# Attention: a third of the modulation in the context tile's units, and the copies of the two heads' probabilities exchanged between ScalarE and VectorE

## The reference

```python
shift1, scale1, gate1, shift2, scale2, gate2 = jnp.split(silu(c) @ w_ada[l] + b_ada[l], 6)   # for c and for c_ctx
h = rms_norm(x, norm1) * (1 + scale1) + shift1
q, k, v, su, sv, cb, cc, cx = jnp.split(h @ w_in, offs, axis=-1)      # 1024 x 2048
q, k = rms_norm per head; latent tokens get rotary positions
s = einsum(q, k_all) * scale; p = softmax(s); attn = einsum(p, v_all) # 8 heads of 64, 2 key heads
merged = [rms_norm(attn), rms_norm(chunk_sgu(su, sv)), rms_norm(conv(cb, cc, cx))]
x = x + gate1 * (merged @ w_out)                                      # 1024 x 1024
h2 = rms_norm(x, norm2) * (1 + scale2) + shift2
x = x + gate2 * hierarchical_moe(h2)                                  # 16 experts, 2 per token
```

## Time and profile before

| | us |
|---|---|
| Median of three runs | 1143.53 (1143.19 to 1144.98) |
| Profiled execution, its own time | 1145.23 |
| Its span in the profile | 1143.4 |
| TensorE busy | 945.5 (83%) |
| VectorE busy | 668.8 (58%) |
| ScalarE busy | 589.6 (52%) |
| GpSimd busy | 264.2 (23%) |
| Mean granted clock of TensorE | 0.908 of the full one |
| Attention, first to last maximum, layer 0 | 168.92 to 271.06 |
| Attention, first to last maximum, layer 1 | 717.91 to 820.27 |

### The profile page before, as it was taken

One profiled execution on the slowest core, in us unless ns is written; L12 is line 12 of the kernel. 1 busy time (PEld: TensorE's weight loads), 2 busy tenths in 40 slices (PEclk: granted clock), 3 DMA queues, 4 the chain that ended last, 5 costly groups with the idle time before them and its releaser, 6 DMA issues.

```text
span 1143.4 us, 14987 instructions
## 1 busy us (share of the span) xinstructions
PE 945.5 (83%) x5232; PEld 742.3 (65%) x5232; DVE 668.8 (58%) x929; ACT 589.6 (52%) x900; POOL 264.2 (23%) x306
## 2 busy tenths in 40 slices
PE   3799989996998599999139999899789849999910
PEld 0488865764886378887128887576578738888710
DVE  0349225654374599998354841455536579998736
ACT  1662235655321388887266322565533328988722
POOL 3024016212140122220330500721204122222033
PEclk9999997999998599999659999799989869999965
DMA  9955213473235999999661321266324539999653
GB/s 323 273 206 211 74 51 148 167 296 113 88 141 181 368 339 410 418 413 321 205 230 61 109 89 29 81 255 245 125 92 148 183 106 380 400 418 410 269 188 124
DMA packets 85951, 248.36 MB, mean 217 GB/s; under 512 B 25644, under 2 KB 30252, under 8 KB 75656
## 3 DMA queue, kind: packets, MB, share of 16 engines
q1 hardware_dynamic: 72760, 209.54, 48.6%
q0 software_dynamic: 11696, 32.86, 8.4%
q10 hardware_dynamic: 1440, 5.24, 1.1%
HBM read 221.07 MB, written 30.21 MB: 220 GB/s over the span
## 4 chain that ended last, share of the span: by engine, by line
PE 72%; DVE 10%; DMA 7%; ACT 5%; issue 4%; POOL 1%; SPq 0%; DVEq 0%; ACTq 0%; POOLq 0%
PE ps L1375 12%; PE ps L1377 12%; PE ps L1376 12%; PE ps L1382 4%; PE ps L1384 4%; PE ps L1383 4%; PE ps L1525 4%; PE ps L1392 4%; PE ps L1510 3%; DMA pool<-in_moe_w 3%; DMA raw<-in_w_ada 2%; PE ps L1499 2%; PE ps L1640 2%; PE ps L1500 2%; DVE wL L1232 1%
## 5 line engine op out<-in xcount | busy, mean ns | idle before, releaser
L1375 PE MATMUL ps<-wH,actH 128*128 128x512 f32 x608 | 248.8, 409 | 13.6 <-DVE actL L1321 12.2
L1377 PE MATMUL ps<-wH,actL 128*128 128x512 f32 x608 | 242.2, 398 | 0.0
L1376 PE MATMUL ps<-wL,actH 128*128 128x512 f32 x608 | 241.3, 397 | 0.0
L1232 DVE TENSOR_TENSOR wL<-raw,wH 128x2048 fp32r<-128x2048 f32 x64 | 146.1, 2283 | 11.4 <-ACT wH L858 11.2
L1375 PEld LDWEIGHTS ps<-wH,actH 128*128 128x128 f32 x608 | 117.4, 193 | 38.3 <-issue 13.3
L858 ACT ACTIVATE wH<-raw 128x2048 fp32r<-128x2048 f32 x64 | 122.2, 1910 | 27.6 <-DMA raw<-in_moe_w 27.6
L1377 PEld LDWEIGHTS ps<-wH,actL 128*128 128x128 f32 x608 | 116.8, 192 | 26.1
L1376 PEld LDWEIGHTS ps<-wL,actH 128*128 128x128 f32 x608 | 117.4, 193 | 22.8
L1382 PE MATMUL ps<-wH,actH 128*128 128x512 f32 x256 | 105.3, 411 | 8.2 <-DVE actL L1310 5.3
L1112 DVE TENSOR_REDUCE nmax<-ps 128x1 f32<-128x640 f32 (+1 forms) x80 | 57.1, 714 | 80.7 <-PE ps L1500 80.5
L1384 PE MATMUL ps<-wH,actL 128*128 128x512 f32 x256 | 102.2, 399 | 0.0
(11 more groups left out here) (226 smaller groups left out, 1576.8 us busy)
## 6 DMA issues: line engine op xcount, KB each, us to landing
raw<-in_w_ada SPq DMA_DIRECT2D x48, 1024.0 KB, 7.9
raw<-in_moe_w SPq DMA_DIRECT2D x96, 512.0 KB, 7.6
raw<-in_w_in SPq DMA_DIRECT2D x16, 1024.0 KB, 9.0
raw<-in_moe_w SPq DMA_DIRECT2D x16, 1024.0 KB
pool<-in_moe_w SPq DMA_DIRECT2D x32, 512.0 KB
pool<-in_moe_w SPq DMA_DIRECT2D x16, 1024.0 KB, 11.5
ys<-pool SPq DMA_DIRECT2D x32, 512.0 KB, 10.4
raw<-in_w_out SPq DMA_DIRECT2D x8, 1024.0 KB, 8.2
```

Of the source, the lines that this page charges most:

```text
L1232: dve.tensor_tensor(wL[:, i, :], mraw[parity][i], f32(wH[:, i, :]), ALU.subtract).then_inc(sem(f"m_lo{i}"), 1)
L1375: pe.matmul(out, aH, wH[:, slot_, cols_], start=first, stop=False)
L1376: pe.matmul(out, aH, wL[:, slot_, cols_], start=False, stop=False)
L1377: return pe.matmul(out, aL, wH[:, slot_, cols_], start=False, stop=last)
```

## The change

- `ADA_AT`: the sixteen modulation units of attention were a third list in tile 1 (two each in units 10 and 11, one each in 12 to 15) and in tile 3 (units 26 to 31). After the change eight are in the context tile (one each in units 2 to 5, two each in 6 and 7) and eight in tile 2 (units 18 to 23). The pieces are complete in units 7 and 23 instead of 15 and 31.
- Piece 1 and its bias move to a region that holds the `sgu_w` weights until they are transposed, and the bias is added in place. Its load on GpSimd moves from after the convolution to before it. `piece_out` of piece 1 and the bias load of piece 2 move before the first statistics; the latter waits for the convolution instead of piece 1.
- The copy of the transposed probabilities of odd heads goes from VectorE to ScalarE, behind the copy of the output, and that of even heads from ScalarE to VectorE, behind the maximum.
- Weight unit w 8 is split in unit 33 instead of 36, and w 9 in unit 37 instead of the merge's chunk 1.

```diff
--- before.py
+++ after.py
@@ -184,8 +184,9 @@
         frow = tabs[:, :, :, :, :].rearrange("p t a b d -> p (t a b d)")[:, 0:D]
-        piece = [misc[:, 0:N], aux[:, 2560:3072], aux[:, 2560:3072]]
-        bpiece = [misc[:, N:2 * N], aux[:, 3072:3584], aux[:, 3072:3584]]
+
+        piece = [misc[:, 0:N], misc[:, 768:1280], aux[:, 2560:3072]]
+        bpiece = [misc[:, N:2 * N], misc[:, 768:1280], aux[:, 3072:3584]]
         mraw = [[raw[:, 0, :], raw[:, 1, :], raw[:, 2, :]],
@@ -236,9 +237,9 @@
         none, third = (0,) * NH, (0, 0, 2, 2, 1, 1, 1, 1)
-        ADA_AT = none + third + none + third + none
+        ADA_AT = (0, 0, 1, 1, 1, 1, 2, 2) + none + third + none + none
         PIECE_AT = [u for u in range(NT * NH) if ADA_AT[u] and sum(ADA_AT[:u + 1]) % KD == 0]
-        W_AT = {36: 8}
+        W_AT = {33: 8, 37: 9}
         def ada_bank(l, q):
@@ -469,9 +470,9 @@
             def bias_in(l, q):
                 if q == 1:
+                    pl.wait_ge(sem("sgT_psum"), at("sgT_psum", l, 1))
+                elif q == 2:
                     pl.wait_ge(sem("conv_done"), at("conv_done", l, 1))
-                elif q == 2:
-                    pl.wait_ge(sem("piece_done"), at("piece_done", l, q))
                 for j in range(4):
                     c = q * U + j * N
                     pl.dma_start(bpiece[q][32 * j:32 * j + 32, :], I["b_ada"][l, c:c + N].partition_broadcast(32)).then_inc(sem("bias_in"), 16)
@@ -501,6 +502,7 @@
                     c = 8 * (i % 2)
                     rstd(stat[:, 16 + c:16 + c + n], stat[:, 32 + c:32 + c + n], n, HD, sem("ssqk"), at("ssqk", l, i + 1), sem("rqk"))
+                bias_in(l, 1)
                 tap = lambda w: cw[:, w, :].unsqueeze(1).to_broadcast([P, NT, 256])
                 pl.wait_ge(sem("shifted"), at("shifted", l, 96))
                 pl.wait_ge(sem("taps_loaded"), at("taps_loaded", l, 32))
@@ -525,11 +527,10 @@
                     link(pl.tensor_scalar(stat[:, c:c + 2], stat[:, c:c + 2], 1.0 / 256, EPS, ALU.mult, ALU.add))
                     pl.tensor_tensor(stat[:, c + 16:c + 18], stat[:, c:c + 2], nhalf[:, 0:2], ALU.pow).then_inc(sem("rstd3b"), 1)
-                bias_in(l, 1)
+                piece_out(l, 1)
+                bias_in(l, 2)
                 rest_stats(0)
                 attn_stats(0)
-                piece_out(l, 1)
-                bias_in(l, 2)
                 rest_stats(1)
                 attn_stats(1)
                 rest_stats(2)
@@ -765,16 +766,16 @@
                 q_out(0, 1)
                 q_hi(1)
                 for u in range(NT * NH + 4):
-                    if u % 2 == 0 and 2 <= u < NT * NH + 2:
+                    if u % 2 and u >= 5:
+                        oT_out((u - 5) // 2)
+                    if u % 2 and 3 <= u < NT * NH + 2:
                         w = u - 2
                         keys = 5 * P if w >= NH else P
                         act.wait_ge(sem("pT_psum"), at("pT_psum", l, w + 1))
                         if w >= 4:
                             act.wait_ge(sem("pv"), at("pv", l, w // 2 - 1))
-                        act.activation(pT[w // 2 % 2][:, 0, 0:keys], flat[:, 4 * N:4 * N + keys], ACT.Copy).then_inc(sem("pT"), 1)
-                    elif u % 2 and u >= 5:
-                        oT_out((u - 5) // 2)
+                        act.activation(pT[w // 2 % 2][:, 1, 0:keys], flat[:, 4 * N:4 * N + keys], ACT.Copy).then_inc(sem("pT"), 1)
                     if u < NT * NH:
                         t, h = divmod(u, NH)
                         keys = 5 * P if t else P
@@ -807,8 +808,6 @@
                     on = cols[:, k:k + 1]
                     act.activation(actHk[:, k, 0:512], ps[:, 5 + 2 * (k % 2), :], ACT.Identity, scale=on).then_inc(sem("mT_hi"), 1)
                     act.activation(actHk[:, k, 512:640], ps[:, 6, 0:P], ACT.Identity, scale=on).then_inc(sem("mT_hi"), 1)
-                    if k == 1:
-                        split_hi(9)
                 for i in range(10, 12):
                     split_hi(i)
@@ -953,9 +952,7 @@
                 dve.wait_ge(sem("ada_read"), at("ada_read", l, KD * (q + 1)))
                 dve.wait_ge(sem("bias_in"), at("bias_in", l, 64 * (q + 1)))
-                if q == 2:
-                    dve.wait_ge(sem("piece_out"), at("piece_out", l, 64))
-                elif l:
+                if l:
                     dve.wait_ge(sem("piece_out"), at("piece_out", l, 0))
                 dve.tensor_tensor(piece[q], ps[:, ada_bank(l, q), :], bpiece[q], ALU.add).then_inc(sem("piece_done"), 1)
@@ -1110,14 +1107,14 @@
                         if u >= 2:
                             dve.wait_ge(sem("prob"), at("prob", l, u - 1))
                         dve.tensor_reduce(nmax[:, u % 2:u % 2 + 1], flat[:, 2 * N * (u % 2):2 * N * (u % 2) + keys], X, ALU.max, negate=True).then_inc(sem("nmax"), 1)
-                    if u % 2 and 3 <= u < NT * NH + 2:
+                    if u % 2 == 0 and 2 <= u < NT * NH + 2:
                         w = u - 2
                         keys = 5 * P if w >= NH else P
                         dve.wait_ge(sem("pT_psum"), at("pT_psum", l, w + 1))
                         if w >= 4:
                             dve.wait_ge(sem("pv"), at("pv", l, w // 2 - 1))
-                        dve.tensor_copy(pT[w // 2 % 2][:, 1, 0:keys], flat[:, 4 * N:4 * N + keys]).then_inc(sem("pT"), 1)
+                        dve.tensor_copy(pT[w // 2 % 2][:, 0, 0:keys], flat[:, 4 * N:4 * N + keys]).then_inc(sem("pT"), 1)
                     if u % 2 and u >= 5:
                         pair_out((u - 5) // 2)
                     if u in W_AT:
@@ -1142,8 +1139,6 @@
                     dve.scalar_tensor_tensor(out=actLk[:, k, 512:640], in0=ps[:, 6, 0:P], scalar=on,
                                              in1=f32(actHk[:, k, 512:640]), op0=ALU.mult, op1=ALU.subtract
                                              ).then_inc(sem("mT_lo"), 1)
-                    if k == 1:
-                        split_lo(9)
                 for i in range(10, 12):
                     split_lo(i)
```

## The result

The changed kernel takes 1153.51 us in the median of five runs, against 1144.77 for the kernel before in its five: 1.0086 of the time, 95% interval 1.0068 to 1.0103, so 9 to 10 us slower (8.7 by the medians, 9.8 by the ratio). The profiled execution has a span of 1151.1 us, 7.7 more than before. My range ended at 1151.5 and my forecast was no change.

What follows compares the result with a forecast made beforehand. TensorE, with 72% of the chain, was taken to bound the kernel. Modulation -2.25, splits +3.5 and tail -0.55 gave +0.7 us a layer, +1.4 in all: 1144.9 us, no change that could be told, range 1138 to 1151.5.

Steps and rivals of the forecast that it cites:

- The context tile: Eight modulation units enter it; first latent maximum at 189.6 instead of 181.61, 8.0 us lost a layer (bounds 4.5 to 12).
- the splits' term for the clock: Tile 4: 1.2 falls of the clock for 1 now, 0.3 us a layer.
- Tile 1: Becomes plain when its modulation leaves: 15.2 us instead of 23.85, 8.65 gained a layer.
- Copies exchanged: Pairs without modulation: 4.56 to 4.29 us, 0.27 off each; queries' low part 0.5 off in tiles 1 and 2 without modulation.
- Modulation moved: Context and latent tiles: 8.0 us lost, 8.65 and 1.6 gained, so 2.25 gained a layer.
- rival 2: Clock stays low through the context tile: 6.0 us a layer slower, 1157 us; chance 0.08.
- the 10 that I had named as a sign of being wrong: Prediction called wrong if the context tile grows by under 5 or over 10 us.
- Rival 3: Context tile's last load at 188.2 and a clock fall for each stall: 1.8 us a layer slower, 1148.5; chance 0.14.
- Splits: Tile 4: TensorE stands 3.5 us in one piece; 3.5 lost a layer, and nothing gained in the merge.
- Rival 1: Second split, in unit 37, is cheap: 1140.7 us at half price, 1136.5 at none; chance 0.26.
- Tail: Last copy goes to ScalarE while VectorE divides the pair before: 0.55 us gained a layer (0 to 0.8).
- Bias load, GpSimd's and SyncE's queues: Earlier bias load covered by GpSimd's wait for shifted rows, SyncE's loads not late, later GpSimd issues cost nothing.

Runs made afterwards that it cites:

- e6_ex_mod: Kernel before with the copies exchanged and the modulation moved, splits as before (unit 36 and merge): 1136.5 us, 0.9931 of the kernel before.
- e7_short_loads: Kernel before with copies exchanged and modulation moved, loads of modulation units 12 to 15 cut to one eighth of their bytes: 1128.1 us, 0.9855.
- e4_w9_back: The changed kernel with w 9 split in the merge again, w 8 still in unit 33: 1144.5 us, 1.0001 of the kernel before.
- e1_exchange: Kernel before with only ScalarE's and VectorE's copies exchanged: 1131.1 us, 0.9890 of the kernel before.
- e5_ex_33: Kernel before with the copies exchanged and w 8 split in unit 33 instead of 36: 1139.4 us, 0.9961 of the kernel before.
- e11_ex_34: Kernel before with the copies exchanged and w 8 split in unit 34 instead of 36: 1132.7 us, 0.9892 of the kernel before.
- e2_modulation: Kernel before with only the modulation moved, with piece 1's new places and GpSimd's new order: 1152.6 us, 1.0073 of the kernel before.
- e10_even: The changed kernel with its two splits one unit later, in units 34 and 38: 1149.1 us, 1.0051 of the kernel before.

## Why the prediction was wrong

Step by step, with the sum of +0.7 a layer against +5.4 and +5.1. Two steps failed. The context tile came out 2.2 and 1.5 over its term, because the clock fell again in the waits for the last loads. And the splits' term for the clock, "1.2 falls of the clock for 1", was too small: the clock fell behind both splits, and the second fall shows in the tail, 1.7 and 2.0 over its term. Tile 1 adds 0.7 and 0.5.

*Copies exchanged.* Right. A plain pair took 4.27 where I had 4.29 (4.56 before). The transposes of two even units, with ScalarE's copy of the odd unit between, in the changed kernel's list of instructions (start, us of it, engine and line, operation, out <- in; in brackets what it waited for and how long):

```profile
237.56 0.73 PE L1505 MATMUL ps<-ident,pool 128*128 128x128 f32 x5
...
240.20 0.74 PE L1505 MATMUL ps<-ident,pool 128*128 128x128 f32 x5
...
240.98 0.71 ACT L778 ACTIVATE pool<-ps 128x640 f32<-128x640 f32 x1 [1.12 <-PE ps L1505]
...
241.83 0.73 PE L1505 MATMUL ps<-ident,pool 128*128 128x128 f32 x5
```

*Modulation moved.* This step failed in the size of two terms, the context tile and what follows it. TensorE's part went as forecast and better: unit 8 of the modulation at 172.12 took 1.94, and the clock was back by 174.6 already, so rival 2 did not happen. The early clock was partly luck, as the last section shows. But then it waited for each of the last loads:

```profile
172.12 1.94 PE L1387 MATMUL ps<-raw,cpad 128*32 128x512 f32 x8
...
174.64 1.06 PE L1387 MATMUL ps<-raw,cpad 128*32 128x512 f32 x8
...
182.39 1.07 PE L1387 MATMUL ps<-raw,cpad 128*32 128x512 f32 x8 [1.35 <-DMA raw<-in_w_ada]
...
184.91 1.94 PE L1387 MATMUL ps<-raw,cpad 128*32 128x512 f32 x8 [0.83 <-DMA raw<-in_w_ada]
...
188.44 1.94 PE L1387 MATMUL ps<-raw,cpad 128*32 128x512 f32 x8 [1.60 <-DMA raw<-in_w_ada]
...
190.31 0.80 PE L1494 MATMUL ps<-actH,actL 128*128 128x512 f32 x1
```

1.35, 0.83 and 1.60: the last load came at 188.4, just past the 188.2 that bounded my range, where I had taken 187.7. What I had not seen is that the clock falls again in those waits (at 184.6, until 191.4): the last two modulation units took 1.94 each and the first wide scores ran slow, so the first latent maximum was at 191.75 and not at 189.6. The earlier trace rows shows just that, and I read it loosely. There the unit right behind the wait of 3.03 still took 1.07, and the slow one (1.94) is the next, behind a further wait of 1.41: the fall came with the second, shorter wait. Those rows also fold the four loads into one line. The loads landed up to 9.5 us after their own issue there, and up to 9.2 here (the view of the loads' line, those four before and the fifth to eighth of layer 0 after):

```profile
DMA to landing us min/median/max: 4.9/7.7/9.5
...
DMA to landing us min/median/max: 4.8/6.9/9.2
```

e6_ex_mod and e7_short_loads show the loads' share, 5.1 of some 10 in layer 0. Tile 1 came out 0.7 longer than taken. In layer 0 the context tile's 10.15 lies just over the 10 that I had named as a sign of being wrong. Rival 3, loads and falls at their dear end, was nearest in kind, but its 1.8 a layer were too few.

*Splits.* The price of the wait was right and its cause was: TensorE stood 3.54 and 3.55, where I had 3.5, and tile 4 grew by 3.7 and 4.0 for 3.5.

```profile
255.19 1.91 ACT L649 ACTIVATE wH<-raw 128x2048 fp32r<-128x2048 f32 x1
...
257.13 2.29 DVE L984 TENSOR_TENSOR wL<-raw,wH 128x2048 fp32r<-128x2048 f32 x1 [2.65 <-ACT wH L649]
...
260.07 0.82 DVE L1117 COPY pool<-ps 128x640 f32<-128x640 f32 x1
...
261.03 1.30 PE L1505 MATMUL ps<-ident,pool 128*128 128x128 f32 x5 [3.54 <-DVE pool L1117]
...
264.74 2.15 PE L1520 MATMUL ps<-pool 128*64 128x128 f32 x20
...
275.55 0.74 PE L1505 MATMUL ps<-ident,pool 128*128 128x128 f32 x5 [3.55 <-DVE pool L1117]
```

That the merge's split was hidden was right too (e4_w9_back: nothing lost by putting it back). Rival 1, a cheap second split, is refuted. Wrong was the clock's part, 0.3 for "1.2 falls of the clock for 1". The clock fell behind each of the two splits in each layer (low from 259.7 and from 276.7 in layer 0), and the value matmuls behind them took 2.15 and 2.14 instead of 1.31. Before, it fell once in this stretch (from 266.7). What the step also did not see is that the exchange had made the split in unit 36 cheaper, by 1.0 and 2.6 us, and the new units throw that away. e1_exchange, e5_ex_33 and e11_ex_34 show it.

*Tail.* The sign came out wrong: +1.1 and +1.4 for -0.55. The term itself was right: with the exchange alone the tail is 12.6 and 12.5 for 13.2 and 13.5 (e1_exchange). But the split in unit 37 ends 1.4 us before the last maximum, and the clock, low after its wait, makes the transposes of the first pair behind it 1.30 instead of 0.74 and its value matmuls 2.14 instead of 1.31:

```profile
277.17 1.30 PE L1505 MATMUL ps<-ident,pool 128*128 128x128 f32 x5 [0.42 <-ACT pool L778]
...
278.40 2.14 PE L1520 MATMUL ps<-pool 128*64 128x128 f32 x20
```

The tail of the change and that of e4_w9_back, with w 9 back in the merge (layer 0, columns as in the earlier trace rows), differ by 1.9 in length and by 2.4 in TensorE's busy time, at a mean clock of 0.79 and 0.96:

```profile
275.32:289.65 14.33, 9.02 (x69) 6.84 (x69) 5.95 (x17) 5.40 (x15) 3.19 (x7) 0.79 0.30 113
...
273.46:285.91 12.45, 6.62 (x69) 4.99 (x67) 5.78 (x16) 4.68 (x13) 3.20 (x7) 0.96 0.15 53
```

*Bias load, GpSimd's and SyncE's queues:* nothing of them shows among TensorE's waits in attention.

*Outside attention* I had no term. There the executions differ by up to 3 us in the stage from the projection to the routing, with the time that the clock is low in it (over the whole execution the clock was low for 213.2 us before, 195.5 in e1_exchange, 214.1 in e5_ex_33). Which part of that belongs to a kernel and which to an execution stays open. In the changed kernel's layer 0 the projection was 0.6 longer than before (49.39 against 48.82 in the earlier trace rows), with the clock low for 1.2 us more at its start; at the last router matmul both stand at 75.8.

## What to carry to other kernels

When two engines take turns at work that one of them must also interrupt for a long operation, look which engine has the next item on the waiting chain: exchanging their turns can move the cheap places for the long operation by one, and places that were chosen before have to be chosen anew. Before moving work into a hole, count how much of it is already on the chip: four of the eight modulation units were, and the other four brought their loads' pace with them and a slow clock. Count a fall of the clock for each long wait that a change adds, as here for two of 3.5 us a layer. A change of several parts whose sum comes out near nothing should be taken apart before it is kept or dropped: one of these three was worth 1.1% and the other two hid it.

## What the runs showed of the hardware that I had not expected

With modulation units between its small matmuls, TensorE's granted clock rose again inside the context tile, where before it had stayed low until 184.7 though TensorE was busy by its rows from 177.9 on the earlier trace rows. How soon differs between executions: 2.2 us after the first modulation unit had begun in the change (172.12, clock up at 174.3), and 6.0 in e4_w9_back, whose code is the same up to there. Its first two units, and the third at the full clock:

```profile
173.16 1.93 PE L1391 MATMUL ps<-raw,cpad 128*32 128x512 f32 x8
...
175.87 1.94 PE L1391 MATMUL ps<-raw,cpad 128*32 128x512 f32 x8
...
179.22 1.06 PE L1391 MATMUL ps<-raw,cpad 128*32 128x512 f32 x8
```

In layer 0, e6_ex_mod is like the first (2.4); e2_modulation, e7_short_loads and e10_even are like the second (6.0 to 6.3). In the change the clock fell again at 184.6, behind waits of 1.35 us and of 0.83 (just ending) between modulation units.

Four loads of 1 MB issued at 174.1, 175.8, 177.6 and 179.2 landed 4.8, 6.6, 7.2 and 9.2 us after their issue, so 3.5, 2.5 and 3.5 apart.
